# Two-layer hybrid decoder step on eight cores: another order of the first loads, transposes by tile, layer 1's loads moved forward, other transfer rates in the list scheduler

## What is computed

```python
h = rms_norm(x, norm_g)                         # D_MODEL = 1024
p = h @ w_in                                    # 1024 x 3456
a_val, a_gate, a_z, b_h, b_b, b_c, b_z, c_u, c_v, c_z = split(p)   # widths 384 x7, 256 x3
a   = a_val * sigmoid(a_gate)
y_a = silu(layer_norm(causal_dwconv(a, width 31) + bias)) * silu(a_z)
y_b = b_b * causal_dwconv(b_c * b_h, width 3) * silu(b_z)
y_c = c_u * chunk_mix(layer_norm(c_v)) * silu(c_z)                 # 128 x 128 causal mix per head
x   = x + concat(y_a, y_b, y_c) @ w_out                            # 1024 x 1024
```

## Time and profile before

| | |
|---|---|
| median of 3 runs | 609.36 us (607.63 to 609.94) |
| profiled execution, its own time | 613.45 us |
| its span on core 1, the slowest | 611.6 us |
| spans of cores 0 to 7 | 602.7, 611.6, 607.4, 599.5, 609.5, 598.7, 607.7, 599.1 us |
| TensorE (PE) busy on core 1 | 582.4 us, 95% of the span |
| VectorE (DVE), ScalarE (ACT), GpSimd (POOL) busy | 453.0, 259.8, 94.7 us |

### The profile page before, as it was taken

One profiled execution on the slowest core, in us unless ns is written; L12 is line 12 of the kernel. 1 busy time (PEld: TensorE's weight loads), 2 busy tenths in 40 slices (PEclk: granted clock), 3 DMA queues, 4 the chain that ended last, 5 costly groups with the idle time before them and its releaser, 6 DMA issues.

```text
span 611.6 us, 12509 instructions; the slowest of 8 cores (598.7 to 611.6 us)
## 1 busy us (share of the span) xinstructions
PE 582.4 (95%) x5002; PEld 330.3 (54%) x5002; DVE 453.0 (74%) x874; ACT 259.8 (42%) x467; POOL 94.7 (15%) x162
## 2 busy tenths in 40 slices
PE   7799998999999999899986999999999999999895
PEld 3545444466556656565642455545565665665552
DVE  2387955678886866587646967889987977876895
ACT  4345623234722732273327213732373274253463
POOL 3500501110110110011043020122011111200101
PEclk9899999999999999899998999999999999999999
DMA  8999997642683594789689989574146336607402
GB/s 180 180 152 222 168 190 128 178 74 70 111 203 52 122 145 142 174 183 229 136 152 214 184 123 250 148 144 156 48 125 141 126 108 154 167 31 108 105 1 103
DMA packets 71737, 86.00 MB, mean 141 GB/s; under 512 B 18944, under 2 KB 60096, under 8 KB 71680
## 3 DMA queue, kind: packets, MB, share of 16 engines
q1 hardware_dynamic: 48560, 60.78, 38.9%
q0 software_dynamic: 18752, 19.93, 24.8%
q10 hardware_dynamic: 4368, 4.51, 3.0%
HBM read 77.77 MB, written 29.81 MB: 176 GB/s over the span
## 4 chain that ended last, share of the span: by engine, by line
PE 83%; DMA 7%; DVE 5%; ACT 2%; issue 1%; SPq 1%; POOL 0%; DVEq 0%; POOLq 0%; ACTq 0%
PE pb L450 76%; PE pb L451 6%; DMA hst<-st_aT 3%; DMA w_in_sb<-w_in 3%; DMA xr<-x_scr 2%; PE pb L620 1%; DVE xr L418 1%; ACT tmp L409 1%; DVE xr L430 1%; SPq L440 1%; DVE xr L977 1%; DVE W L506 0%; DVE h_tm L430 0%; ACT L409 0%; ACT h_fm L409 0%
## 5 line engine op out<-in xcount | busy, mean ns | idle before, releaser
L450 PE MATMUL pb<-h_fm,w_in_sb 128*128 128x384 bf16 (+3 forms) x2032 | 371.6, 342 | 10.6 <-DVE a_t L430 4.6
L450 PEld LDWEIGHTS pb<-h_fm,w_in_sb 128*128 128x128 bf16 x2032 | 197.1, 99 | 170.4 <-issue 5.8
L409 ACT ACTIVATE tmp<-pb 128x384 f32<-128x384 f32 (+2 forms) x110 | 56.4, 518 | 146.7 <-PE pb L450 143.5
L450 PE MATMUL pb<-w_out_sb,mix 128*128 128x512 bf16 (+1 forms) x544 | 115.9, 379 | 0.0
L450 PEld LDWEIGHTS pb<-w_out_sb,mix 128*128 128x128 bf16 (+1 forms) x544 | 51.5, 98 | 61.6 <-issue 0.8
L409 ACT ACTIVATE tmp<-xr 128x1024 bf16<-128x1024 f32 (+2 forms) x52 | 53.8, 1035 | 66.5 <-DVE xr L418 41.6
L418 DVE TENSOR_TENSOR xr<-pb,xr 128x512 f32<-128x512 f32 (+1 forms) x72 | 47.6, 687 | 30.1 <-PE pb L450 29.9
L563 POOL TENSOR_SCALAR rstd<-ss 128x1 f32<-128x1 f32 (+1 forms) x46 | 14.8, 321 | 252.1 <-ACT tmp L409 251.8
L430 DVE SCALAR_TENSOR_TENSOR tmp<-z_ext,pc,tmp 128x384 f32<-128x384 bf16 (+1 forms) x60 | 37.7, 640 | 7.7 <-ACT tmp L409 7.1
L418 DVE TENSOR_TENSOR mix<-tmp 128x384 bf16<-128x384 f32 (+2 forms) x50 | 29.3, 590 | 14.6 <-ACT tmp L409 14.5
L430 DVE SCALAR_TENSOR_TENSOR h_tm<-xr,rstd,ng_b 128x1024 bf16<-128x1024 f32 (+1 forms) x30 | 37.7, 1277 | 1.9 <-POOL rstd L564 1.1
(11 more groups left out here) (108 smaller groups left out, 507.2 us busy)
## 6 DMA issues: line engine op xcount, KB each, us to landing
A<-a_scr SPq DMA_DIRECT2D x32, 309.0 KB, 7.9
w_in_sb<-w_in POOLq DMA_DIRECT2D x17, 512.0 KB, 23.2
xr<-x_in SPq DMA_DIRECT2D x16, 512.0 KB, 8.6
x_scr<-xr SPq DMA_DIRECT2D x16, 512.0 KB, 7.0
xr<-x_scr SPq DMA_DIRECT2D x16, 512.0 KB, 6.1
y_o<-xr SPq DMA_DIRECT2D x15, 512.0 KB, 3.1
w_out_sb<-w_out POOLq DMA_DIRECT2D x4, 1024.0 KB, 19.8
w_in_scr<-w_in POOLq DMA_DIRECT2D x7, 512.0 KB, 9.2
```

Source lines behind the costliest of these rows:

```text
L409: S.add("act", lambda e: e.activation(out=out, in_=in_, func=func, **kw), reads=reads, writes=writes, cost=170 + 0.833 * free_size(out) + ...
L450: return lambda e: e.matmul(out, lhsT, rhs, start=start, stop=stop)
```

## The change

1. The plan's transfer rates go from 220 and 250 bytes per ns (SyncE, GpSimd) to 150 and 200, and the start-up time from 1300 to 2000 ns. That alone gives every engine another order in places.
2. First loads: `consts` first; tile 1 of `x` on ScalarE's queue beside tile 0 on SyncE's; pieces 0 and 1 of `w_in` without waiting; tile 2 of `x` and piece 2 after tile 1 has landed; tile 3 after tile 2; pieces 3 to 12 after tile 3 and piece 2.
3. The first block is normalised, transposed and moved into `h_fm` tile by tile (`T_in`: one DVE operation of 5 x 128 columns and three ACT operations of 128), and the first-half projections of all three c precede the second half's.
4. `hist_dma` ahead of `w_out` in block 0; block 0's `LN_out` and block 2's `x` loads move into block 1; `T_tile` in stages B and C of block 0.
5. Layer 1's parameters are loaded in block 2 of layer 0 and half prepared there (`params_early`); only the two `cbias` DMAs (four before) stay at the layer's end. `x` of layer 1 from its second block on is loaded in stage B of the block two before, not at the start of the block before.
6. In the last block the final norm of block 3's tiles (`fin`) is done after `stage_stats`, not in `stage_O`.

```diff
-    RATE = {"sp": 220.0, "pool": 250.0, "act": 150.0}
+    RATE = {"sp": 150.0, "pool": 200.0, "act": 150.0}
...
-        for t in blocks[0].ids:
-            load_x(0, t)
-            if t == 0:
-                dma("sp", cst[:], consts, [], ["cst"])
-                dma("act", pc[:], pcols, [], ["pc"])
-            if t == 1:
-                xmark = [S.ops[-1].idx]
+        dma("sp", cst[:], consts, [], ["cst"])
+        load_x(0, 1, (), "act")
+        xmark = [S.ops[-1].idx]
+        load_x(0, 0)
+        dma("act", pc[:], pcols, [], ["pc"])
...
         for i in range(len(PIECES)):
-            load_win(0, i, xmark if i else ())
+            if i == 2:
+                load_x(0, 2, xmark)
+                xmark = [S.ops[-1].idx]
+                load_x(0, 3, xmark)
+            load_win(0, i, xmark if i > 1 else ())
+            if i == 2:
+                xmark = [o.idx for o in S.ops[-2:]]
...
+        for j in range(4):
+            hs = hslot()
+            H_norm(0, blocks[0].ids[j], 128, hs, False, ev if j > 1 else ())
+            T_in(j, hs)
...
+            if j == 1:
+                ev = [max(o.idx for o in S.ops if o.eng == "act")]
+                params_dma(0, mark())
+                cbias_dma(0, mark())
+                dummy(8)
+                A_half(0, 0)
+                A_half(1, 0)
+            if j == 2:
+                A_half(2, 0)
+        for c in range(3):
+            A_half(c, 1)
...
             if c == 0:
-                LN_out(l, blk, mark())
+                hist_dma(l, mark())
                 for hf in range(2):
                     load_wout(0, hf, mark())
...
-            if not tail and oi > 1:
+            if not tail and 1 < oi < 5:
                 for t in nxt[1].ids:
                     load_x(nxt[0], t, mark())
...
-            stage_O(*prev)
+            fins = stage_O(*prev, tail)
...
+            if l == 0 and blk.i == 2:
+                params_dma(l + 1, mA)
...
                 if c == 0 and tail:
                     stage_stats(l, blk)
+                    for f in fins:
+                        f(mark())
+                if c == 1 and 4 <= oi < len(order_b) - 2:
+                    for t in order_b[oi + 2][1].ids:
+                        load_x(1, t, mark())
...
             if final:
-                params_dma(l + 1, mark())
+                cbias_dma(l + 1, mark())
```

More of the change, by code:

```diff
@@ L1102, in build_program @@
         wb = balloc()
[L1103 to L1105 removed]
+        pe([mm(pbank[wb][:, :], ones_bf[:], mix[:, 0, :], True, True) for _ in range(22)], ["ones", ("mix", 0)],
+           [pk(wb)], 22 * 300)
         brel(wb)
@@ L1130, in A_half @@
+        pre = [(balloc(), balloc()) for _ in range(3)]
         def A_half(c, hv):
             for b, col in zip(pre[c], (C_AV, C_AG)):
-                proj_part(b, col + 128 * c, 256 * hv, 256 * hv + 256, hfm(hv))
-        T_half(0)
-        ev = [max(o.idx for o in S.ops if o.eng == "act")]
-        m0 = mark()
-        H_norm(0, blocks[0].ids[2], 128, hslot(), False)
-        H_norm(0, blocks[0].ids[3], 128, hslot(), False, ev)
-        params_dma(0, m0)
-        S.add("pe", lambda e: [mm(pbank[pre[0][0]][:, :], ones_bf[:], mix[:, 0, :], True, True)(e) for _ in range(8)],
-              reads=["ones", ("mix", 0)], writes=[pk(pre[0][0])], cost=8 * 216, after=m0)
@@ L1150, in build_program, with dummy @@
-        A_half(1, 0)
-        A_half(0, 1)
-        A_half(1, 1)
+                proj_part(b, col + 128 * c, 256 * hv, 256 * hv + 256, hfm(hv) + [("hf3", k) for k in range(8) if hv])
+        def dummy(n):
+            S.add("pe", lambda e: [mm(pbank[pre[0][0]][:, :], ones_bf[:], mix[:, 0, :], True, True)(e) for _ in range(n)],
+                  reads=["ones", ("mix", 0)], writes=[pk(pre[0][0])], cost=n * 216, after=mark())
+        for j in range(4):
+            hs = hslot()
+            H_norm(0, blocks[0].ids[j], 128, hs, False, ev if j > 1 else ())
+            T_in(j, hs)
+            if j == 0:
+                dummy(3)
+            if j == 1:
[7 more added lines that the diff above has]
+                A_half(2, 0)
```

134 lines of the change are left out of this document (61 added, 73 removed).

## The result

The changed kernel takes 618.16 us (median of 4 runs, 617.12 to 619.12). Its ratio to the kernel before, run on the same chip, is 1.0151 with a 95% interval of 1.0116 to 1.0185. The forecast was 604, the range 596 to 611: the time lies outside. Its profiled execution took 619.12 us; core 6 is the slowest with a span of 617.1, and the eight cores lie between 603.6 and 617.1.

A forecast was written before the change was run, and what follows sets the result against it. TensorE, busy 582.4 of 611.6 us, bounds the kernel, with the front living from its weight stream. 613.45 + 4.5 - 1.7 - 7.0 - 1.0 = 608.25, less 4.1: 604.2, forecast 604, range 596 to 611.

The forecast's parts named there:

- PE stands almost without waits in the steady part: Steady part: the new rates reorder all engines a little, costed at nothing, bounds -1 and +2 us.
- First block: Front: PE waits for piece 2 until 26.0 us, group A ends at 36.5, not 32.1; +4.5 us.
- the upper bound of +6.7: First block: piece 2 lands at 27.4 us with a second wait of 0.88, so group A ends at 38.8.
- With the engines already full: Front: DMA engines full from 7 to 67 us, so another order moves a landing only by what it overtakes.
- The stream: Weight pieces after piece 2: 3 to 4.5 us late, but PE late by 4.4 itself; +0.1 near 70 us.
- Second block: Shifts at 93.48 us: histories loaded ahead of `w_out` remove PE's wait of 1.69; -1.7 us, bounds 0 and -3.1.
- Layer change: Early loads of `x` remove ScalarE's idling and PE's waits; -7.0 us, bounds -2 and -7.5.
- The rival that it would turn into another wait: Layer change: loads of `x` held by block 3's stores, ScalarE's norms still late, only 2 us won; 609.2; chance 0.18.
- Last block: Three final norms moved behind `stage_stats` remove PE's wait of 1.19 at 576.76 us; -1.0, bounds -1.2 and +2.6.
- The bound of +2.6: Last block: the case where two of the three moved final norms delay the last tiles.
- The slower rival: Weight stream decides, not made up before 67 us; front +10, layer change only -4, 613.7 us; chance 0.10.
- The base: Profiled execution before, 613.45 us against median 609.36: a stall and slow clock taken as accident, 4.1 taken off.

The follow-up runs named there:

- e4: Changed kernel with the plan's old figures put back (220 and 250 bytes per ns, 1300 ns): ratio 1.0067 to the kernel before.
- e7: Kernel before with the plan's new figures alone (150 and 200 bytes per ns, 2000 ns): ratio 1.0070.
- e14: The kernel of e11 with the plan's new figures (150 and 200 bytes per ns, 2000 ns) put back: ratio 0.9939 to the kernel before.
- e8: Changed kernel with the old front, old plan figures, `LN_out` held by its mark and GpSimd's preparation not held: ratio 0.9974 to the kernel before.
- e1: Changed kernel with piece 2 waiting for tile 1 of `x` and pieces 3 to 12 for tile 3 alone: ratio 1.0045 to the kernel before.
- e12: The kernel of e10 with the changed front, loosened as in e1, in place of the old front: ratio 1.0019 to the kernel before.
- e10: The kernel of e8 with layer 1's first-block loads of `A` waiting for the `h_tm` stores: ratio 0.9900 to the kernel before.
- e5: Changed kernel with block 0's `LN_out` entered where it was before, held by its mark: ratio 1.0130 to the kernel before.
- e9: Changed kernel with layer 1's first-block loads of `A` waiting for the last store of `h_tm`: ratio 1.0085 to the kernel before.
- e11: The kernel of e10 with the transposes of block 1's tiles at their old places in block 0: ratio 0.9854 to the kernel before.

## Why the prediction was wrong

The step that failed most is the one sentence "PE stands almost without waits in the steady part, so I cost that at nothing, bounds -1 and +2". Between the slowest cores the terms miss by +7.7 at layer 1's second block, +4.7 in the second block, +3.0 in the first, +1.3 in the last and -1.4 at the layer change; with -0.4 for the rest that is 14.9, from 604.2 to the 619.12 of the profiled execution. The largest miss lies at a place for which the prediction has no term but that sentence. The new rates put another order on every engine: e4 takes 0.8% of the time back by the old figures alone, e7 and e14 show 0.7% and 0.8% from the new ones alone, in two other kernels. The rates are not the only way to that order, though: e8 has the old ones and the early loads of `x`, and there all four stores stand behind the loads of `A`. The order was there to be read before any run: SyncE's rows at the layer change were looked at for the loads of `x` only, and the two more stores that had come to stand behind four loads a few rows further on were not.

**First block, forecast +4.5, measured +6.9 in the median and +7.5 between the slowest cores.** Right in kind, and over the upper bound of +6.7 either way. The path held: PE's wait for piece 2 ended at 23.0 to 29.0 us (26.9 in the median, forecast 26.0), and the shifts came 9.0 to 12.8 later (10.9, forecast 10.5). Mis-sized was the landing on the slow cores, 28.9 on core 6. A part of the +6.9 is the base: +4.4 was counted from core 1's 32.14, the latest of the eight cores, whose median is 30.8. One reading was wrong: I took piece 2 to wait for tile 1's landing, and the text on the change says so too. The order's row shows `d_sp_2`, tile 2's landing, and GpSimd issues it at 16.26 for that reason. e1, which lets it go after tile 1 and the later pieces after tile 3 alone, has it 3.5 us earlier and wins 1.1%. "With the engines already full" doesn't hold around that landing, where core 6 shows 0.11 from 27 to 33 us, but PE waits for none of the pieces behind that gap. I had costed `T_in` at nothing under cover of the wait for piece 2. e1 and e12 take that cover away, and then PE waits for tile 3, itself held by tile 2: the rest of the changed front costs e12 1.2% against e10, and how much of this is the hold and how much the tile-wise order stays open.

**The stream, forecast level at 70 us.** No wait for a piece after 30 us: it was late, and PE was later.

**Second block, forecast -1.7, measured +2.9.** The histories' wait went as forecast, on all cores. Two waits came that the prediction did not have: 2.7 for `a_t` (GpSimd and VectorE together, and the three channel groups close behind one another) and 2.2 for `nv`, with 3.4 us at a granted clock of 0.50 behind it on seven of the eight cores. e5 shows that the second isn't had back by moving `LN_out` alone: PE then waits 2.0 to 2.9 for `h_tm`, also from VectorE; e8, with the front, the rates, `LN_out` and the preparation as before, has neither.

**Layer change, forecast -7.0, measured -6.7 in the median and -8.4 between the slowest cores.** Right by mechanism and by size. The rival that it would turn into another wait looked for that wait at the norms' `x`, held by the stores; this did not happen, ScalarE idles at most 1.58 there. Another wait came one block later, at the transposes: +3.1 in the median, +7.7 between the slowest cores, and e9 takes it away by moving four loads.

**Last block, forecast -1.0, measured +0.6 before the last output projection and +1.9 behind it.** The bound of +2.6 held the case; the value was taken from the wait that I could see and not from VectorE's 15.03 of 15.29 us.

**The slower rival** had a chance of 0.10 and the right sign. Its mechanism, the weight stream deciding at 67 us, is not what happened: no such wait is there. The gain at the layer change that it cut to -4 was full.

The base held: 4.2 us of the profiled execution before were an accident, and with them the 5.7 between the two profiled executions become 9.9, near the 8.8 between the medians.

## What to carry to other kernels

When an order comes from a scheduler, a change of its cost table is a change of the program: read the new order on every queue for stores that have come behind loads, above all where a small buffer (two slots of `h_tm` here) waits for the store. Holding a transfer until another has landed is only free if something else fills the queue; a chain of such holds empties it. And a wait removed is worth nothing until the next consumer has been followed: here -7 us at one place gave up to 7.7 back one block later, and with four loads moved, and the front, the rates, `LN_out`, the preparation and the transposes of block 1 as before (e11), what is left of the change is 1.5% faster than the kernel before.
